# A modulation matrix in four column groups of TensorE, and a recurrence without its reciprocal: one change to a hybrid S5, RG-LRU and PEER block on one core

## The reference, cut to what matters

```python
mod_l = split(silu(c)     @ w_ada + b_ada, 6)      # w_ada: 2048 x 12288, 100 MB
mod_c = split(silu(c_ctx) @ w_ada + b_ada, 6)      # only parts 0 and 1 are used
n_lat = rmsnorm(x,   g_norm1) * (1 + mod_l[1]) + mod_l[0]
n_ctx = rmsnorm(ctx, g_norm1) * (1 + mod_c[1]) + mod_c[0]
z = n @ w_in                                       # u | v | gate | two output gates
ya = s5_mixer(u)                                   # state space, 64 groups of 16 channels
# RG-LRU, in both directions, for each of 1024 channels:
r, i = sigmoid(x @ w_r + b_r), sigmoid(x @ w_i + b_i)
log_a = -8 * r * softplus(-lambda);  a = exp(log_a)
h_t = a_t * h_(t-1) + sqrt(-expm1(2 * log_a)) * i_t * x_t
# merge, w_out, residual with mod_l[2]; then norm with mod_l[3:5], PEER
# (16384 experts, top 16 of 8 heads per token), residual with mod_l[5], norm
```

## Time and profile before

| | |
|---|---|
| runs | 2724.91 us median of 3 (2724.87 to 2724.92) |
| profiled execution | 2728.4 us, of which span 2726.6 us |
| PE busy | 2208.6 us (81%) |
| DVE busy | 1518.0 us (56%) |
| POOL, ACT busy | 1011.7 us, 420.9 us |
| DMA | 793.52 MB, mean 291 GB/s |

### The profile page before, as it was taken

The page is one execution under the profiler, slowest core; times in us unless marked ns, Lnnn a source line. Parts: engine busy times, 40 slices in busy tenths (PEclk is TensorE's granted clock), DMA queues, the critical chain, the costliest instruction groups (busy, mean ns, idle before and its releaser), DMA issues.

```text
span 2726.6 us, 21339 instructions
## 1 busy us (share of the span) xinstructions
PE 2208.6 (81%) x7864; PEld 1271.2 (47%) x7864; DVE 1518.0 (56%) x2413; ACT 420.9 (15%) x804; POOL 1011.7 (37%) x905
## 2 busy tenths in 40 slices
PE   5989779978888886979988888777777777777777
PEld 2434334867666665868764344222222222222223
DVE  6414662189999992112285555555665565665441
ACT  3013340012222221000110011111011101111101
POOL 3000000445555551010054643555555455455541
PEclk9999889998889887989999999999999999999999
DMA  9831112876876773575399999999999999999995
GB/s 269 289 124 62 37 60 86 189 237 207 253 220 208 232 237 107 184 254 165 124 362 411 418 399 422 421 421 422 421 422 421 421 416 422 422 422 421 421 411 202
DMA packets 315207, 793.52 MB, mean 291 GB/s; under 512 B 25736, under 2 KB 243088, under 8 KB 247264
## 3 DMA queue, kind: packets, MB, share of 16 engines
q0 software_dynamic: 81600, 561.36, 50.6%
q1 hardware_dynamic: 223712, 225.55, 26.5%
q10 hardware_dynamic: 9792, 5.25, 0.8%
HBM read 778.40 MB, written 9.50 MB: 289 GB/s over the span
## 4 chain that ended last, share of the span: by engine, by line
DMA 32%; PE 16%; POOL 3%; DVE 2%; issue 2%; ACT 0%; DVEq 0%; ACTq 0%; POOLq 0%
DMA vb<-in_peer_v,eidx 30%; PE ps L1537 8%; PE ps L1484 4%; PE ps L1509 3%; DMA rows<-in_peer_u,eidx 2%; POOL vb L1252 1%; POOL rows L1252 1%; POOL mT L1252 1%; DMA cut<-in_peer_sub_keys 0%; DVE rows L1444 0%; PE ps L1494 0%; PE ps L1519 0%; DVE mT L1444 0%; DVE oh L1407 0%; DVE oh L1405 0%
## 5 line engine op out<-in xcount | busy, mean ns | idle before, releaser
L1537 PE MATMUL ps<-vb,diag 128*128 128x512 f32 x2048 | 952.2, 612 | 291.6 <-DMA vb<-in_peer_v,eidx 287.1
L1537 PEld LDWEIGHTS ps<-vb,diag 128*128 128x128 f32 x2048 | 376.8, 192 | 864.5 <-DMA vb<-in_peer_v,eidx 453.9
L1444 DVE CUSTOM_DVE_ANT_0 rows<-rows,f 128x2048 f32<-128x2048 f32 x170 | 387.8, 2291 | 335.4 <-DMA rows<-in_peer_u,eidx 335.0
L1252 POOL DMA_INDIRECT vb<-in_peer_v,eidx x256 | 369.7, 1444 | 503.0 <-PE ps L1537 485.7
L986 PE MATMUL ps<-nT,w_ring 128*128 128x256 f32 (+1 forms) x1792 | 521.2, 452 | 5.4 <-issue 4.8
L986 PEld LDWEIGHTS ps<-nT,w_ring 128*128 128x128 f32 x1792 | 349.6, 197 | 183.8 <-issue 146.9
L1444 DVE CUSTOM_DVE_ANT_0 mT<-mT,f 128x2048 f32<-128x2048 f32 x86 | 196.4, 2291 | 176.7 <-DMA mT<-in_peer_u,eidx 176.6
L905 DVE SCALAR_TENSOR_TENSOR zu<-w_ring,scol,zu 128x256 f32<-128x256 f32 x448 | 237.5, 594 | 5.9 <-DMA w_ring<-in_w_ada 3.7
L1252 POOL DMA_INDIRECT rows<-in_peer_u,eidx x170 | 205.2, 1207 | 92.8 <-issue 48.2
L1328 ACT ACTIVATE diag<-ident,wgt 128x128 f32<-128x128 f32 x256 | 94.1, 397 | 661.7 <-PE ps L1537 656.4
L1252 POOL DMA_INDIRECT mT<-in_peer_u,eidx x86 | 102.1, 1187 | 214.7 <-DVE eidx L1414 161.4
(11 more groups left out here) (326 smaller groups left out, 1844.0 us busy)
## 6 DMA issues: line engine op xcount, KB each, us to landing
w_ring<-in_w_ada SPq DMA_DIRECT2D x96, 1024.0 KB, 9.1
w_ring<-in_w_in SPq DMA_DIRECT2D x56, 1024.0 KB, 5.2
w_ring<-in_w_out SPq DMA_DIRECT2D x16, 1024.0 KB, 5.3
w_ring<-in_peer_w_query SPq DMA_DIRECT2D x16, 1024.0 KB, 12.1
w_ring<-in_w_proj_a SPq DMA_DIRECT2D x8, 1024.0 KB, 5.4
w_ring<-in_w_proj_b SPq DMA_DIRECT2D x8, 1024.0 KB, 5.4
gates_dram<-gst POOLq DMA_DIRECT2D x16, 256.0 KB, 6.3
big<-big SPq DMA_DIRECT2D x128, 32.0 KB, 5.3
```

Source lines behind the costliest of these rows:

```text
L1252: pool.indirect_dma_start(ring[m % n], None, table, bass.IndirectOffsetOnAxis(ap=eidx[:, i % 3, j:j + 1], axis=0))\
L1444: v.tensor_tensor_reduce(ub[m % n_u], ub[m % n_u], f[:, i // HEADS], 1.0, 0.0, ALU.mult, ALU.add, hd[:, i % 2, j:j + 1]).then_inc(u_used, 1)
L1537: last = pe.matmul(ps[:, 4 * tile + c, :], diag[:, m % NDIAG], vb[m % NV][:, c * 512:(c + 1) * 512], start=(r == 0), stop=(r == HEADS * K ...
```

## The change: what it does

1. **Columns of `w_ada` in four column groups.** A unit of `w_ada` now holds 4 row blocks k of 512 columns (rows of 2 KB, `ada_view`). `scol` becomes 128 x 16 x 32, the two columns followed by 30 of zeros. Matmul k writes 32 partitions of PSUM that begin at 32 (k mod 4), with 512 moving columns, so that four partial sums over k lie in the four quarters of the partitions. The compiled program places them in tiles of 128 rows by 32 columns of the array, at columns 0, 32, 64 and 96.
2. **A selector matmul** adds the four quarters: `sel` (128 x 2) has ones at partitions 32 g + c. ACT copies all 128 partitions of the partial sums to `part`, in the place of the buffer `zu`. For the first 4096 columns `mod_columns` uses 128 columns of `part` as weights and `sel` as moving data; the result comes out with one column of `w_ada` per partition, as `nscale` and `nshift` want it. The store to DRAM, the load back and the late transposition are gone.
3. **In the stages** `modulations` on DVE is gone; PE does `mods` after `s5_params`, and after `s5_states` one selector matmul with the row result for the store.
4. **Recurrence.** q = 2 tanh / (1 + tanh) becomes q = (1 + a a) tanh: one product on DVE and one fused operation in the place of an addition, a reciprocal and a fused operation. `rt`, `ig`, `ag` get three buffers; ACT's `gates(k)` waits for `scans(k-3)`.
5. The eight copies to `pwq` and `pP` on DVE are moved behind the scaling of `nT`.

```diff
+        for q in range(8):            # first columns; 8 + s in stage s
+            for x in range(4):
+                src = w_ada[:, 4 * x:4 * x + 4, q * ADA:(q + 1) * ADA]
...
+def ada_view(slot):
+    return slot.rearrange("p k n -> p (k n)").rearrange("p (k n) -> p k n", n=ADA)
...
# ACT, first columns
-            for c in range(16):
-                mod_rows(A0 + c, c)
+            for q in range(8):
+                act.wait_ge(acc_full, A0 + q + 1)
+                if q >= 2:
+                    act.wait_ge(sel_done, q - 1)
+                act.activation(part[:, q % 2], ps[:, (A0 + q) % 2, :], ACT.Copy).then_inc(acc_free, 1)
# ACT, recurrence
-                b = k % 2
-                if k >= 2:
-                    act.wait_ge(lru_done, k - 1)
+                b = k % 3
+                if k >= 3:
+                    act.wait_ge(lru_done, k - 2)
# DVE, recurrence
-                step(tsc(ltmp, rt[:, b], 1.0, None, ALU.add))
-                step(v.reciprocal(ltmp, ltmp))
-                stt(rt[:, b], rt[:, b], 2.0, ltmp, ALU.mult, ALU.mult).then_inc(q_ready, 1)
+                step(tt(ltmp, ag[:, b], ag[:, b], ALU.mult))
+                stt(rt[:, b], ltmp, 1.0, rt[:, b], ALU.add, ALU.mult).then_inc(q_ready, 1)
# DVE, stages
                 if s < NSTAGE:
-                    modulations(s, (0, 1))
                     build_m(s)
-                    modulations(s, (2, 3))
# PE
             def mods(a):
                 free(a)
-                for h_ in range(2):
-                    w = unit(pe, n[0])
+                for x in range(4):
+                    w = ada_view(unit(pe, n[0]))
                     n[0] += 1
-                    for k in range(UK):
-                        last = pe.matmul(ps[0:2, a % 2, 0:COLS], sc[:, h_ * UK + k, :], w[:, k, :],
-                                         start=(h_ + k == 0), stop=(h_ * UK + k == KD - 1))
-                    last.then_inc(unit_done if h_ == 0 else acc_full, 1)
+                    for j in range(4):
+                        last = pe.matmul(ps[32 * j:32 * j + 32, a % 2, :], scol[:, 4 * x + j, :], w[:, j, :],
+                                         start=(x == 0), stop=(x == 3))
+                    last.then_inc(ada_used if x < 3 else acc_full, 1)
+            def mod_columns(q):
+                pe.wait_ge(acc_free, A0 + q + 1)
...
+                for i in range(4):
+                    c = 2 * (4 * q + i)
+                    last = pe.matmul(ps[:, 7, c:c + 2], part[:, q % 2, i * P:(i + 1) * P], sel[:], start=True, stop=True)
+                last.then_inc(sel_done, 1)
...
                     s5_params(s)
+                    mods(S0 + 4 * s + 2)
                 else:
                     s5_out(s - 2)
                 if 1 <= s <= NSTAGE:
                     s5_states(s - 1)
                 if s < NSTAGE:
-                    pe.wait_ge(ada_used, 4 * s + 4)
-                    for e in range(2):
-                        last = pe.matmul(ps[0:1, a % 2, :], ones[:], ada_acc[:, :, e, :], start=(e == 0), stop=(e == 1))
-                    last.then_inc(acc_full, 1)
+                    pe.wait_ge(acc_free, a)
+                    pe.matmul(ps[0:1, a % 2, :], sel[:, 0:1], part[:, s % 2], start=True, stop=True)\
+                        .then_inc(acc_full, 1)
```

More of the change, by code:

```diff
@@ L33 @@
 COLS = 256
+ADA = 512
 UK = 8
@@ L102, in build @@
             plan_pair(w_in, 3 * W // COLS + s, acc_full, acc)
[L103 to L107, removed]
+            acc += 2
+            plan_ada(8 + s, acc - 1)
         for c in range(W // COLS):
@@ L122, in load_unit @@
                 eng.wait_ge(units[u - RING][1], units[u - RING][2])
-            eng.dma_start(w_ring[:, u % RING], units[u][0]).then_inc(w_in_sem[u % RING], 16)
+            slot = w_ring[:, u % RING]
+            if units[u][0].shape[1] == 4:
+                slot = ada_view(slot)
+            eng.dma_start(slot, units[u][0]).then_inc(w_in_sem[u % RING], 16)
         def unit(pe, u):
@@ L178, in mixer @@
         sqt = nT.rearrange("p k n -> p (k n)")[:, 0:D]
-        ada_acc = zu.rearrange("p b s c -> p (b s c)").rearrange("p (j e n) -> p j e n", j=2, e=2)
-        ones = sb("ones", [P, 1])
+        part = zu.rearrange("p b s c -> p b (s c)")
         gst = sb("gst", [P, 2, 2, T])
@@ L342, in _, with store_mods @@
                             .then_inc(bd_in, 16)
[L344 to L356, removed]
+            def store_mods(s):
+                pool.wait_ge(acc_free, S0 + 4 * s + 4)
+                pool.dma_start(mods_dram[0:1, (8 + s) * ADA:(9 + s) * ADA], modst[0:1, s % 2]).then_inc(mods_out, 16)
+                pool.wait_ge(mods_out, 16 * (s + 1))
             for k in range(KW):
@@ L477, in _ @@
                 act.activation(xt[i], xt[i], ACT.Copy, scale=xss[:, 4 + i:5 + i]).then_inc(xn_done, 1)
[L479 to L483, removed]
-                               ACT.Copy).then_inc(acc_free, 1)
-            for c in range(16):
-                mod_rows(A0 + c, c)
+            for q in range(8):
[3 more added lines that the diff above has]
+                act.activation(part[:, q % 2], ps[:, (A0 + q) % 2, :], ACT.Copy).then_inc(acc_free, 1)
             act.wait_ge(norm_ready, 1)
@@ L1002, in lag_zero @@
                         last.then_inc(kz_full, 1)
-            for c in range(16):
-                mods(A0 + c)
-                if c == 11:
+            for q in range(8):
+                mods(A0 + q)
+                if q == 5:
                     lag_zero()
-            pe.wait_ge(mrow_in, 16 * 2)
-            pe.wait_ge(mrow_back, 16 * 4)
-            pe.wait_ge(s5_setup, 4)
-            pe.transpose(ps[:, 2, 0:112], mrow[:], ident[0:112, 0:112]).then_inc(mcol_tr, 1)
+                if q >= 1:
+                    mod_columns(q - 1)
+            mod_columns(7)
             pe.wait_ge(xn_done, 4)
@@ L1099, in _ @@
                 if s < NSTAGE:
-                    two = columns(S0 + 3 * s, T, 2 * T)
+                    two = columns(S0 + 4 * s, T, 2 * T)
                     next(two)
```

142 lines of the change are left out of this document (73 added, 69 removed).

## The result

The changed kernel takes 2661.8 us (median of 4 runs, 2659.9 to 2668.4), beside 2724.9 for the kernel before on the same chip: a ratio of 0.9775, 95% interval 0.9763 to 0.9786. It is 63 us faster, half of the 129 us that the forecast's working gave, and 7 us above the upper end of its range. The profiled execution took 2662.0 us, span 2659.9, against 2728.4 before.

What follows compares the result with a forecast made beforehand. The first 1060 us were taken as bound by PE and DMA, then ACT and DVE in turn, then DVE in the stages; -37 - 49 - 43 = -129 us on 2728.4, said as 2600 us, range 2562 to 2655.

Steps and rivals of the forecast that it cites:

- What bounds the kernel: First 1060 us: PE and DMA near their end in first columns, ACT and DVE in turn in recurrence, DVE in stages.
- The price of a chunk: 16 `w_ada` matmuls in four column groups: 3.8 us taken, between 3.4 all at once and 13.6 one after the other.
- L1057's pairs: Row-half matmuls at L1057: 1.71 us instead of 3.0, read as two float32 matmuls in different tiles running side by side.
- both rivals on it: Chunk price: passes in order, 6.8 us, 2626 in all, chance 0.13; groups one after the other, 13.6 us, 2747, chance 0.14.
- First columns: Up to v's columns: DMA limits, `lag_zero` covered, last unit in at 132, 5 us behind it; -37 us, bounds -25 and -48.
- Recurrence: Columns of v with gates: PE sets the pace, gates 17.17 us apart instead of 27.67; -49 us, -42 if some waits stay.
- Stages: Stages: 28.3 us each, 2.5 less than now; with stage 0 -43 us together, bounds -80 and -19.
- my two bounds: Scan's end in a stage: `h_done` between 7.1 and 11.9 us behind the states, so PE waits 0 to 4.1 us.
- the late unit: Stages: the next column block's second unit waits for the chunk's first unit, 5 us before it is wanted; called tight.
- Sum: Whole kernel: -37 - 49 - 43 = -129 us on the profiled 2728.4; 2600 said for the median.
- the third rival: Stages stay at 30.8 us through crowded scan, late tight load and lower clock; 2634 us in all, chance 0.13.
- the tail: Behind the last stage: the chain through the last scans and every distance from `w_out` on stay the same.

Runs made afterwards that it cites:

- experiment 8: The kernel before with only the wait of the stages' store moved ahead of the next store: 2765.0 us, 1.0151 of before.
- experiment 9: Experiment 1's kernel with the lag-zero matmuls issued after the second group of columns instead of the sixth: 2593.5 us, ratio 0.952.
- experiment 1: The changed kernel with POOL's wait for its store of modulations moved ahead of the next such store: 2594.7 us, 0.9528 of before.
- Experiment 6: The changed kernel with two buffers for each gate tile instead of three: 2678.2 us.
- experiment 2: The changed kernel with TensorE waiting for the second unit of `w_in` only where it reads it: 2681.5 us.
- experiments 10 and 11: Filler matmuls ahead of TensorE's wait for the scan: three in the changed kernel, 2640.7 us; four in experiment 2's kernel, 2633.3 us.
- experiment 3: The changed kernel with the edits of experiments 1 and 2 together: 2603.5 us.
- experiment 7: The changed kernel with GpSimd's six operations building the next projection left out in stages 2 to 16: 2591.7 us, ratio 0.9506.
- experiment 4: The changed kernel with all `w_ada` matmuls in one column group, one after the other: 2762.9 us, 1.014 of before.

## Why the prediction was wrong, by its steps

- **What bounds the kernel.** Right for the first two parts. For the stages I named VectorE, and it was so: it is busy 30.08 of the 30.85 us of one stage (experiment 8).
- **The price of a chunk.** 3.8 us taken, 3.64 measured. The forecast from L1057's pairs came true, and both rivals on it fell. The Trainium skill (TensorE: Matmul & The Clock Gate, Part 3: Packing small matmuls, The mechanism) says that matmuls start and end in strict order and that weight loads overlap only where the row group differs; here the row group is the same and 3.8 of 4 groups' worth of concurrency is measured (3.64 against 13.92 us), with the loads inside it. The measurement decides. The 2.38x that the Trainium skill (the same part, Measured speedup vs the span model) gives for three groups was too low a guide for four of float32.
- **First columns.** -37 forecast, -32.3 measured. The rate was better than I took (386 against 355 GB/s), but `lag_zero` was not covered (experiment 9), the last unit came about 1.5 us later than 132, and the tail behind it was 7.5 us, not 5: the last four matmuls took 1.9 us where I had 0.6, and sixteen weight loads at half clock 3.58 where I had eight in 1.0. Up to here experiment 1 is the same program, and in its profile v's first block starts at 151.75 instead of 153.61, so some 2 of the 4.7 us missing can be spread between executions.
- **Recurrence.** -49, exactly, with starts 17.17 us apart. Experiment 6 agrees with the 21.7 us for two buffers.
- **Stages: the step that failed.** I forecast 28.3 us a stage, 25.8 of TensorE's work at full clock and 2.5 of waiting; it was 31.84. The 25.8 were right as work (experiment 1: 27.1 with 1.2 of waiting). Two terms were not. The first is the wait. I took 2.5 us, between a scan that is quiet and one that is always crowded, though before, the scan was crowded in all fourteen stages that had both scan and `build_pb`. It is crowded now too: the outputs can't start before 11.8 us behind the states, the upper of my two bounds, and TensorE stands still for 3.6 us a stage on the mean, 1.5 for the late unit and 2.1 for the scan. That the wait ahead of L1097 is 2.45 us in the stage shown, as forecast, is luck: the late unit, which I had called tight and priced at nothing, hides the rest of it, and without it that wait is 3.8 (experiment 2). Only in two of the fifteen stages is the late unit's wait, 2.6 us, the one that counts. The second is the clock. I priced TensorE at full clock although the row of 8.84 us lay before me: the second block takes 8.8 us on the mean where I had 6.8, and the outputs 3.2 (up to 5.1) where I had 2.7. Some 1.1 us of waiting and 2.5 of clock make up the 3.5 us between 28.3 and 31.84.
- **The rivals.** The third one named all of this: a crowded scan, a late load, the lower clock; I gave it 0.13, on the argument that "the crowded scan alone leaves 29.9 us". With the waits filled, the stages of experiments 10 and 11 in which the clock stays up last 29.8 us, so the figure was right; but the scan does not come alone, as the clock falls with the wait. Even that rival was too kind: it kept the stage at 30.8, and it grew by 1.1 us.
- **Sum.** 4.7 us from the first columns, 55 from the stages with what follows u, 2.9 from the tail, in all 63 us short of the forecast. The 0.86 for faster came true; the range, whose upper end was the third rival with 20 us of margin, was too narrow since that rival had no room for being worse than it said. Of the tail's 2.9 us, 2.2 lie between the last sum and the last outputs (L1091's last start is 1048.5 before, L1097's is 981.4 after, 67.1 us apart instead of 69.3). Most of that, 1.6, is no loss: before, the last sum came later behind the states; the outputs after it start 67.7 us apart. 0.6 are outputs at half clock. The other 0.7 are not explained.

## What to carry to other kernels

When work leaves an engine, ask which waits it had hidden: here the crowded scan ended just as TensorE came from its wait for the products, and with the products gone TensorE waits for the scan. A wait on a store that was useful before (experiment 8: its move costs 41 us) cost 67 us after. Price TensorE behind every wait that stays with the clock that the trace shows behind such waits, not with full clock; waits of 3.6 to 3.8 us a stage cost another 1.4 when they came in two pieces and some 3 when they came in one. And where one engine's shortened chain ends in a wait, read what runs on GpSimd beside VectorE's part of it.

## What the runs showed of the hardware beyond the expected

- Four float32 matmuls in four column groups with the same 128 rows run at 3.8 times the speed of one after the other: 3.64 against 13.92 us for 16 matmuls of 512 columns.
- VectorE's operations on two SBUF tensors beside GpSimd's tensor operations: 256 elements 1.2 to 1.4 us instead of 0.43, the scan 2.0 instead of 1.22, products 0.91 instead of 0.42 each. The Trainium skill (SBUF — State Buffer, Who interferes with whom) says that a VectorE instruction with two SBUF inputs contends with a GpSimd one that reads SBUF, and calls the shared ports an exclusive lock. The step-by-step rows agree, and they add a price: a chain of eleven short operations goes from 5.6 to 10.3 us.
- The granted clock fell behind single waits of 2.4 to 3.8 us, and in experiment 3 in stages with no wait above 0.6 us. The length of the wait alone does not decide it: in experiment 7 a first block took 8.8 us behind a wait of 1.79 and 7.1 behind one of 2.12. What does was not isolated.
- With `w_ada` in rows of 1 KB the DMA engines moved 345 GB/s, with rows of 2 KB 386. That the rows are the reason is not shown: before, TensorE was never idle in that stretch and could hold the loads back, and in experiment 4, with 2 KB rows and TensorE again never idle, the same 30 us show 317 GB/s.
